# A third of the expert weight loads on ScalarE's DMA queue, one gather moved up, and experts 0 and 1 in the row of all others

## What is computed

```
gi = argmax(gl, axis=-1)                  # one of 4 groups of experts
wv, wi = lax.top_k(pe, 2)                 # two of the 8 experts inside it
for e in range(32):
    a = t @ w_gate[e]                     # 1024 x 512
    u = t @ w_up[e]                       # 1024 x 512
    out = out + combine[:, e:e + 1] * ((silu(a) * u) @ w_down[e])   # 512 x 1024
y = _rmsnorm(x + out, final_norm_g)
```

## Time and profile before

| | us |
|---|---|
| median of 3 runs | 795.86 |
| lowest, highest | 795.11, 798.78 |
| the profiled execution, its time | 791.86 |
| the profiled execution, its span | 790.1 |
| PE busy | 678.9 |
| DVE busy | 268.9 |
| ACT busy | 160.7 |
| POOL busy | 89.2 |
| bytes moved by DMA | 246.56 MB |

### The profile page before, as it was taken

The page is one execution under the profiler, slowest core; times in us unless marked ns, Lnnn a source line. Parts: engine busy times, 40 slices in busy tenths (PEclk is TensorE's granted clock), DMA queues, the critical chain, the costliest instruction groups (busy, mean ns, idle before and its releaser), DMA issues.

```text
span 790.1 us, 9766 instructions
## 1 busy us (share of the span) xinstructions
PE 678.9 (86%) x3306; PEld 332.9 (42%) x3306; DVE 268.9 (34%) x555; ACT 160.7 (20%) x314; POOL 89.2 (11%) x159
## 2 busy tenths in 40 slices
PE   6999989999986888999799987877777878875897
PEld 2488878954546433343233322322222222222232
DVE  7698993374575211112111111111111111111055
ACT  3577410322422011111011110110001010010023
POOL 4100000000001021121011121111111111111000
PEclk9999999999997899999999999998999899897999
DMA  9422026387228989999999999999999999999552
GB/s 334 170 107 108 1 79 252 108 337 335 84 88 327 341 314 402 407 391 406 399 418 404 404 413 410 414 405 414 410 389 402 424 408 419 389 402 423 229 208 108
DMA packets 29575, 246.56 MB, mean 312 GB/s; under 512 B 6578, under 2 KB 7090, under 8 KB 16592
## 3 DMA queue, kind: packets, MB, share of 16 engines
q1 hardware_dynamic: 22784, 233.95, 73.8%
q0 software_dynamic: 5280, 8.20, 3.1%
q10 hardware_dynamic: 1456, 3.62, 1.2%
HBM read 235.65 MB, written 19.20 MB: 323 GB/s over the span
## 4 chain that ended last, share of the span: by engine, by line
PE 57%; DMA 26%; DVE 9%; issue 3%; ACT 3%; POOLq 0%; SPq 0%; POOL 0%; ACTq 0%; DVEq 0%
PE psA L1305 31%; PE psB L1305 25%; DMA mem<-in_w_gu 24%; DVE mem L676 4%; DMA mem<-hn_d,mem 2%; ACT mem L622 1%; ACT front_c L609 1%; DVE mem L815 1%; PE psA L1310 1%; DVE mem L827 1%; DMA mem<-in_w_vb 1%; DVE mem L857 0%; DVE mem L858 0%; PE psB L1310 0%; ACT mem L557 0%
## 5 line engine op out<-in xcount | busy, mean ns | idle before, releaser
L1305 PE MATMUL psA<-mem 128*64 128x512 f32 (+8 forms) x1380 | 329.9, 538 | 43.3 <-DMA mem<-in_w_gu 24.2
L1305 PE MATMUL psB<-mem 128*64 128x512 f32 (+6 forms) x1242 | 274.5, 537 | 42.8 <-DMA mem<-in_w_gu 27.1
L1305 PEld LDWEIGHTS psA<-mem 128*64 128x64 f32 (+4 forms) x1380 | 155.5, 158 | 198.6 <-issue 167.8
L1305 PEld LDWEIGHTS psB<-mem 128*64 128x64 f32 (+2 forms) x1242 | 115.4, 154 | 182.8 <-issue 149.2
L676 DVE TENSOR_TENSOR mem<-mem 128x512 f32<-128x512 f32 (+20 forms) x116 | 64.9, 572 | 24.2 <-ACT mem L526 20.1
L1220 POOL DMA_INDIRECT y_d<-front_c,mem x30 | 27.4, 914 | 301.3 <-DVE front_c L1051 301.3
L1067 DVE TENSOR_TENSOR front_c<-front_c,psB 64x512 f32<-64x512 f32 x15 | 10.3, 690 | 142.3 <-ACT front_c L609 142.3
L1067 DVE TENSOR_TENSOR front_c<-front_c,psA 64x512 f32<-64x512 f32 x15 | 10.3, 689 | 141.2 <-ACT front_c L609 141.2
L1215 POOL DMA_INDIRECT mem<-hn_d,mem x34 | 33.5, 986 | 101.1 <-DMA hn_d<-mem 71.6
L609 ACT ACTIVATE front_c<-psA 64x512 f32<-64x512 f32 x15 | 8.8, 589 | 146.7 <-PE psA L1305 146.7
L609 ACT ACTIVATE front_c<-psB 64x512 f32<-64x512 f32 x15 | 8.8, 589 | 136.8 <-PE psB L1305 136.8
(11 more groups left out here) (232 smaller groups left out, 384.6 us busy)
## 6 DMA issues: line engine op xcount, KB each, us to landing
mem<-in_w_gu SPq DMA_DIRECT2D x64, 2048.0 KB, 31.4
mem<-in_w_down SPq DMA_DIRECT2D x32, 2048.0 KB, 39.5
mem<-in_w_out SPq DMA_DIRECT2D x2, 2048.0 KB, 8.4
y_d<-mem SPq DMA_DIRECT2D x1, 4096.0 KB, 11.8
mem<-y_d SPq DMA_DIRECT2D x8, 512.0 KB, 7.3
mem<-in_x_T SPq DMA_DIRECT2D x8, 260.0 KB, 8.7
mem<-in_w_vb SPq DMA_DIRECT2D x8, 256.0 KB, 8.9
mem<-in_x_prompt SPq DMA_DIRECT2D x4, 512.0 KB, 11.1
```

Of the source, the lines that this page charges most:

```text
L1305: return nc.tensor.matmul(out, lhsT, rhs, start=start, stop=stop, skip_group_check=True)
```

## The change

Six things change.

1. Loads with (q - 10) % 3 == 2, those into a slot that held down weights, leave SP's loop. ScalarE issues them in `tail`, behind its wait for `dn_ps`. These are the units j = 0 of experts 4 to 31, 28 in all. SP's loop now waits only for `gu_half` and `gu_used`.
2. Experts 0 and 1 lose `own=True` on all engines; expert 1's step has the default `before=True`. The wait for `picks_rdy` comes behind step 1.
3. ScalarE's loop over the steps is written out in Python, as slot numbers differ from step to step.
4. In the step of expert 29, POOL issues the gather of expert 30's second tile before the store of expert 28, where expert 29 has no second tile (`early=True`).
5. At the end the tiles go in the order 0, 1, 2, 4, 3. For tiles 2, 4 and 3 PE no longer adds `x2`; VectorE adds it to the kept results (`add_kept`), and the square reads the sum from `x2`.
6. VectorE adds the rows of tiles 0 and 1 before expert 31's product.

```diff
+        LAST_ORDER = (0, 1, 2, 4, 3)
+        LAST_PS = [psA[:, 0:2, :], psA[:, 2:4, :], psB[:, 0:2, :], psA[:, 0:2, :], psB[0:NS, 2:4, :]]
+        IN_PSUM = (0, 1)
...
             for q in range(NSLOT, 3 * NE):
                 e_old, j_old = (q - NSLOT) // 3, (q - NSLOT) % 3
+                if j_old == 2:
+                    continue
                 if e_old == 0 and j_old == 0:
                     sp.wait_ge(gu_half, 1)
-                elif j_old < 2:
+                else:
                     sp.wait_ge(gu_used, e_old + 1)
-                else:
-                    sp.wait_ge(dn_ps, e_old + 1)
                 load(q // 3, q % 3)
...
                 act.wait_ge(dn_ps, s + 1)
+                q = 3 * s + 2 + NSLOT
+                if q < 3 * NE:
+                    slot, _ = place_of(q // 3, q % 3)
+                    act.dma_start(ring[:, slot, :], w_dn[q // 3] if q % 3 == 2 else w_gu[2 * (q // 3) + q % 3]).then_inc(w_full[slot], 16)
                 stored(act, n_stored, u)
...
-            tile_step(0, 0, 0, before=False, own=True)
-            tile_step(1, 0, 1, before=False, own=True)
-            tile_step(2, 0, 0, before=False)
-            with act.Fori(1, NE // 2 - 2) as i:
-                tile_step(i * 2 + 1, i, 1)
-                tile_step(i * 2 + 2, i, 0)
+            tile_step(0, 0, 0, before=False)
+            tile_step(1, 0, 1)
+            tile_step(2, 0, 0)
+            for s in range(3, NE - 3):
+                tile_step(s, (s - 1) // 2, s % 2)
...
+            add_rows(0)
+            add_rows(1)
+            dve.wait_ge(sg_rdy, NE)
+            V.tensor_tensor(hh[0:64, 1, :], sg[64:128, 1, :], psB[64:128, 1, :], ALU.mult).then_inc(h_done, 1)
+            for t in LAST_ORDER[2:]:
+                add_rows(t)
...
+                if early:
+                    x0, x1, x_next = (pool.value_load(xb[0:1, s + k:s + k + 1], min_val=0, max_val=NX) for k in range(3))
+                    with pool.If(x0 >= x1):
+                        with pool.If(x1 < x_next):
+                            fetch_further(x1)
                 if before:
                     store(s - 1, i, 1 - u)
...
             rest(0)
             pe.wait_ge(y_last, 2)
-            pe.wait_ge(y0_ev, NE - 2)
-            pe.wait_ge(y1_ev, NE - 2)
+            kept(0, 0)
             rest(1)
-            kept(0)
-            kept(1)
-            rest(2)
-            kept(2)
-            rest(3)
-            kept(3)
+            kept(1, 1)
+            kept(2, LAST_ORDER[2])
+            kept(3, LAST_ORDER[3])
             pe.wait_ge(f_done, 1)
-            rest(4)
-            kept(4)
+            kept(4, LAST_ORDER[4])
```

More of the change, by code:

```diff
@@ L400, in _ @@
                 sp.wait_ge(y_out[u], 16 * (NE // 2 - 1))
-            for t in range(NT):
+            for t in LAST_ORDER:
                 for c in range(2):
@@ L603, in further, with tile_step @@
                     A(xyst[0:C, 0:512], other[0:64, 0, :], ACT.Copy).then_inc(xx_y0, 1)
-            def tile_step(s, i, u, last=False, before=True, own=False):
+            def tile_step(s, i, u, before=True):
                 ps, other = (psA, psB)[u], (psA, psB)[1 - u]
@@ L614, in tile_step @@
                 further(x0, x1, other)
-                if own:
-                    tail(s, i, u)
             def tail(s, n_stored, u):
@@ L654, in _ @@
                 A(ylast[:, 512 * h:512 * h + 512], psB[64 * h:64 * h + 64, 3, :], ACT.Copy).then_inc(y_last, 1)
-            for t in range(NT):
+            for n, t in enumerate(LAST_ORDER):
                 r = ROWS[t]
-                act.wait_ge(f_ps, t + 1)
-                A(yin[0:r, 2 * t, :].rearrange("p (a n) -> p a n", a=2), LAST_PS[t], ACT.Square, accum_out=fx[0:r, t:t + 1]).then_inc(f_sq, 1)
-                act.wait_ge(f_sq, t + 1)
+                if t in IN_PSUM:
+                    act.wait_ge(f_ps, n + 1)
+                    total = LAST_PS[t]
+                else:
+                    act.wait_ge(f_sum, n + 1 - len(IN_PSUM))
+                    total = x2[0:r, t, :].rearrange("p (a n) -> p a n", a=2)
+                A(yin[0:r, 2 * t, :].rearrange("p (a n) -> p a n", a=2), total, ACT.Square, accum_out=fx[0:r, t:t + 1]).then_inc(f_sq, 1)
+                act.wait_ge(f_sq, n + 1)
                 A(ss[0:r, 2, t:t + 1], fx[0:r, t:t + 1], ACT.Sqrt, scale=1.0 / D, bias=epsc[0:r, :]).then_inc(f_rt, 1)
@@ L1067, in tile_step @@
                 V.tensor_tensor(hh[0:64, u, :], sg[64:128, u, :], ps[64:128, 1, :], ALU.mult).then_inc(h_done, 1)
-                if not last:
-                    xT_copy(s + 1, 1 - u)
+                xT_copy(s + 1, 1 - u)
                 if before:
@@ L1273, in tile_step @@
                         fetch_further(x1)
-                if own:
-                    store(s, i, u)
+                else:
+                    with pool.If(x0 < x1):
+                        with pool.If(x1 < x_next):
+                            fetch_further(x1)
             fetch_first(0)
@@ L1604, in turn_rows, with tile_step @@
                 x_T((psA, psB)[s % 2][:, 0, :], xg[0:C, s % 2, :]).then_inc(xgT_ps, 1)
-            def tile_step(s, before=True, own=False, split=False):
+            def tile_step(s, before=True, split=False):
                 u = s % 2
@@ L1644, in _ @@
             x_T(psA[:, 0, :], xg[0:C, 0, :]).then_inc(xgT_ps, 1)
-            tile_step(0, before=False, own=True, split=True)
+            tile_step(0, before=False, split=True)
             pe.wait_ge(cw3_rdy, 1)
@@ L1650, in _ @@
             ins.then_inc(cw_ps, 1)
+            tile_step(1)
             pe.wait_ge(picks_rdy, 1)
-            tile_step(1, before=False, own=True)
-            tile_step(2, before=False)
-            for s in range(3, NE - 2):
+            for s in range(2, NE - 2):
                 tile_step(s)
```

62 lines of the change are left out of this document (31 added, 31 removed).

## The result

The changed kernel takes 803.11 us (median of 7 runs, 801.38 to 805.0), the kernel before beside it 795.11 (7 runs, 791.09 to 798.78): ratio 1.011, 95% interval 1.0081 to 1.0139. That is 8.0 us more by the medians, where the forecast was 795.7, no change. The time lies inside the stated range (785 to 804) and above the forecast's own 792 to 800. In what follows the times are medians of all executions and the ratios leave out the executions over 1.5% above the fastest of their kernel (811.71 us of two_overtake, 2651.53 us of the kernel before).

A forecast was written before the change was run, and what follows sets the result against it. It took the DMA weight stream up to the landing of expert 29's second gate-up half, then PE's own work and the store, as the bound; 2.3 + 7.9 + 0.9 - 10.4 - 0.9 = -0.2 us gave 795.7 us, range 785 to 804.

The forecast's parts named there:

- Order of landing: Expert 29's second gate-up half: ScalarE's units land ahead of SP's, so PE waits 1.5 units longer, +7.9 us (+6.8 to +10.5).
- Clock after the longer wait: Last wait for weights: two short waits become one, so the half behind runs partly at low clock, +0.9 us (0 to 1.7).
- Experts 0 and 1: Start of the weight stream: three units start at 283.1 us, delaying the stream by +2.3 us (+1.3 to +4.0).
- The second gather: Expert 30's second tile: PE's gather wait (-8.0), slow turn (-0.4) and slow gate-up (-2.0) go, -10.4 us; bound -8.
- What is late next is nothing: Behind the removed gather wait: expert 30's units land 13 us after expert 29's second half, wanted at 19.
- The last stage: Final tiles: VectorE takes three matmul groups' additions from PE, less a full-tile last store, -0.9 us (-1.6 to -0.3).
- y rows are in by then: Ahead of expert 31's product: two row additions, 5 us, fit in the 7 us between the two products.
- Throughput: Weight stream: SP's queue alone keeps DMA share at 1.0 to 1.01, so a second queue gains nothing, 0 us.
- Rival (b): Weight stream: two interleaved streams carry 3.7% less than one, +10 us, 805 us; chance 0.13.
- (d): Expert 30's second tile: the gather's wait only moves, most of the 8 us and the clock return, 804 us; chance 0.07.
- (a): Expert 29's second half: ScalarE's units don't get ahead at PE's cost, +7.9 and +0.9 fall away, 786.9 us; chance 0.20.
- (c): Weight stream: two streams fill what one leaves, 1.7% of 430 us, -7 us, 788 us; chance 0.10.

The follow-up runs named there:

- two_overtake: Kernel before, with only the first gate-up halves of experts 30 and 31 loaded on ScalarE's queue: 802.30 us against 794.66, ratio 1.0093.
- tail_in_order: Changed kernel, with the first gate-up halves of experts 30 and 31 back on SP's queue in their old place: 794.22 us against 793.50, ratio 1.0013.
- gather_only: Kernel before, with only the gather of expert 30's second tile moved ahead of the store of expert 28: 786.77 us, ratio 0.9911.
- queue_only: Kernel before, with only the 28 loads moved to ScalarE's queue and its loop written out: 802.46 us, ratio 1.0104.
- all_on_sp: Changed kernel, with all 96 loads on SP's queue again: 790.76 us against 793.93 for the kernel before, ratio 0.9956.
- gather_hoist: Kernel before, with the earlier gather and VectorE's three loads of expert numbers ahead of the tail of expert 29: 784.01 us against 794.66, ratio 0.9873.
- gather_last: Kernel before, with the earlier gather, VectorE's expert-number loads moved ahead and the new last stage: 787.45 us against 793.50, ratio 0.993.
- stream_two: All computation left out, only the 96 weight units loaded, every third on ScalarE's queue: 481.65 us, against 482.59 on one queue.
- the bare streams: Two runs without computation, only the 96 weight units of 2 MB: 482.59 us on SP's queue alone, 481.65 with every third on ScalarE's.

## Why the prediction was wrong, by its own steps

The forecast was no change and the kernel became slower. The mechanism on which the sum hung, the order of landing, was right, as two_overtake and tail_in_order show, and its term was right in size. Three other steps failed: the last landing was to come 2.3 us later and came 9.6 us later; the second gather was to give 10.4 us, with nothing late behind it, and gave 7.3; the low clock behind the last wait was to cost 0.9 us and cost 3.0. Of these only the second is seen in the medians as well (gather_only, -7.2); the other two rest on the rows of the profiled executions.

- **Order of landing, +7.9.** Right: +7.5 after, 8.3 in queue_only, 7.7 in two_overtake, for ScalarE's unit that lands in 16.5 us (median) beside SP's 35.8 and 43.5. It landed later than the 10.5 us forecast, three times the stream's 5.25 us a unit and not twice, and it had been issued earlier (10.3 us ahead of the half, not 7.2). The two errors cancel, which is luck: 29.2 / 5.25 = 5.6 units remained, where the forecast had 5.5.
- **Clock after the longer wait, +0.9.** Mis-sized. The half took 6.62 us, +3.0, and 5.76 and 6.13 in the two runs with the queue. The bound of 1.7 was taken from a gate-up of two halves behind a wait of 3.27 us; the wait here was 6.18 us. The forecast had one wait of 2.5 to 4 us in each step. From 490 us on the trace has waits of 4.4 to 7.6 us two or three steps apart, and at most 2.3 us in between; the halves behind the long ones took 5.35 to 6.62 us.
- **Experts 0 and 1, +2.3.** Mis-sized in the profile: some 5 us there. The bound of +4.0 allowed 1.7 us for a low clock in expert 1's gate-up; it was expert 0's that met it, for 2.7 us (10.06 against 7.40). Alone the edit costs +2.4 us by the medians, the forecast's size. Expert 0's gate-up took 7.40 us in all_on_sp and tail_in_order, which have the same row, so the edit doesn't bring the low clock with it. The two longest gate-ups stand behind the two longest waits for expert 0's gather (2.01 and 3.00 us); why these were longer is open.
- **A term that was missing.** Of the 9.6 us by which the last landing is late, some 5 are the start's. The rest has one place that the windows show: 0.92 of a full stream at 400 to 420 us, that is 1.6 us. Shortly before, at 387.30, PE had stood 6.07 us for the gather of the other second tile (before 1.68), and so let go of slots late. The gathers' landing after, shortest, median and longest, against the earlier trace rows:

```profile
DMA to landing us min/median/max: 3.7/12.9/18.4
```

  That the second queue slows POOL's transfers was priced only for expert 30's. These gathers are at 12.7 us in queue_only and tail_in_order too, and at 8.8 in all_on_sp, so the loads on ScalarE's queue slow them. The remaining 3 us have no single place; tail_in_order, which has the same dip (0.94), doesn't have all of them. A pace of 404 instead of 406 GB/s would make 2 us of 400, and kernels with one queue differ by more than that (402 to 408).
- **The second gather, -10.4.** Too much by 3.1: -7.3 in the trace, -7.2 by gather_only. The wait went, as forecast. "What is late next is nothing" was the step that failed: VectorE's register loads were late next, and with them the low clock stayed. gather_hoist gets the whole term, -10.3 in its rows up to the end of that gate-up and -10.6 by the medians.
- **The last stage, -0.9.** -1.4 in the trace, -1.1 alone, unresolved; the sign and the size fit. Its "y rows are in by then" held in the changed kernel and failed in gather_last and all_on_sp.
- **Throughput, 0.** Right. Rival (b), with its 3.7%, is excluded as a mechanism by stream_two and by the 404 GB/s after: 805 was near the time for a reason that was not its own, and so was the 804 of (d). The bound in (b) is also wrong in itself: from 795.7 to 799.8 us it takes 1.5%, not 1.1%.
- **Rivals (a), (c), (d)** didn't happen: the half did not start near 706, the stream carries 404 GB/s and not more, and the turn of the second tile has no wait for the gather.

So the forecast's -0.2 us became +11.1 in the spans by +7.3 (landing), -0.4 (order), +2.1 (clock), +3.1 (gather) and -0.5 (last stage), and by -0.3 (idle behind the half). By the medians it was +8.0: some 3 us of the account are particular to the two profiled executions, and which terms they belong to isn't shown. That the time fell inside the stated range is no merit of the sum: the upper end of the range was rival (d)'s.

## What to carry to other kernels

Loads put on a second queue come first, and those left behind come last; so ask of each not when it is issued but which load PE needs next, and keep the last ones before a stretch that only PE bounds in the order of need. When a wait is taken away, look at what ran under its cover on every engine, register loads and branches too, since they are the next thing late. Work moved ahead of a product because "its data is in by then" holds only while the engine ahead stays as slow as it was: the same two additions cost nothing in the changed kernel, and 1.54 and 3.31 us of idle PE, with the low clock behind it, in two quicker ones.

## What the runs showed of the hardware

- A 2 MB load on an empty queue beside a queue with a backlog lands after 13.7 us in the bare streams and 16.5 in the kernel (medians), a load of 2 MB alone after 7.8; those behind the backlog land after 52.6 to 58.3 in the bare stream, where one queue alone has 48.9.
- The bare stream carries 428 GB/s at a share of 1.01, the kernels 402 to 408 at a share of 1.00 to 1.01 (300 to 700 us). The share of busy DMA engines doesn't tell these apart. What takes the 5% wasn't tried.
- Row gathers on POOL's queue land after 8.8 us (median; longest 11.1) beside SP's loads alone, and after 12.9 (18.4) with a third of the loads on ScalarE's queue.
- In all traces of this case, a gate-up half behind a wait for weights of 3.90 us or more (up to 7.74) took 5.1 to 6.6 us where a full-clock half takes 3.65. Behind shorter waits it went either way: 3.65 us behind 3.85 (all_on_sp), 5.35 behind 2.62 (tail_in_order), 3.65 behind 2.46.
- A scatter of 64 rows landed 5.4 us after its issue while weights were still streaming (at 738 us in gather_last), and 2.4 us after it when they were in (at 758 us after the change).
